# Moving expert turns between the phases of a decoder layer's second half

## What is computed

```python
f = lb + (1 - lb) * sigmoid(fa)
oa, S_new = hgrn_chunked(q, 1 - f, i, log(f), S0)
ya = (rms_norm(oa) * silu(ga)) @ w_branch_a
yb = merged_window_attention(q, k, v, caches) @ w_branch_b
x = x + g1 * ((sigmoid(gA) * ya + sigmoid(gB) * yb) @ w_out)
n2 = rms_norm(x) * (1 + sc2) + sh2
...
act = gelu(einsum('td,thkd->thk', n2, u[eidx]))
x = x + g2 * einsum('thk,thkd->td', g * act, v[eidx])
```

## Time and profile before

| | |
|---|---|
| median of three runs | 4373.25 us |
| the profiled execution's own time | 4375.05 us |
| its span, first to last instruction | 4373.3 us |
| mean granted TensorE clock | 0.824 |
| PE, PEld busy | 3063.8 us (70%), 1663.8 us (38%) |
| DVE busy | 2572.8 us (59%) |
| ACT busy | 1940.2 us (44%) |
| POOL busy | 1446.6 us (33%) |
| bytes moved, mean rate | 1454.06 MB, 332 GB/s |

### The profile page before, as it was taken

The page is one execution under the profiler, slowest core; times in us unless marked ns, Lnnn a source line. Parts: engine busy times, 40 slices in busy tenths (PEclk is TensorE's granted clock), DMA queues, the critical chain, the costliest instruction groups (busy, mean ns, idle before and its releaser), DMA issues. The chain is left out here.

```text
span 4373.3 us, 46875 instructions
## 1 busy us (share of the span) xinstructions
PE 3063.8 (70%) x14244; PEld 1663.8 (38%) x14244; DVE 2572.8 (59%) x6558; ACT 1940.2 (44%) x6708; POOL 1446.6 (33%) x1174
## 2 busy tenths in 40 slices
PE   7999877784898998566654686885555556555556
PEld 5677754641553446344432464551111111111111
DVE  2362335377566755584654545467667766766774
ACT  2123431045457844574542225445455555545554
POOL 4453102352332333232211113335244344334432
PEclk9998889886999999666876797887777776777879
DMA  7434245388999999787999988999999999999997
GB/s 281 185 142 138 83 142 179 112 354 335 364 406 377 422 421 401 287 334 274 382 360 361 344 308 312 381 368 386 403 420 420 415 409 420 420 404 419 417 407 308
DMA packets 313887, 1454.06 MB, mean 332 GB/s; under 512 B 41609, under 2 KB 102977, under 8 KB 165282
## 3 DMA queue, kind: packets, MB, share of 16 engines
q0 software_dynamic: 152064, 1107.36, 62.6%
q1 hardware_dynamic: 147118, 336.43, 21.7%
q10 hardware_dynamic: 14452, 7.26, 0.6%
HBM read 1383.55 MB, written 74.57 MB: 333 GB/s over the span
## 5 line engine op out<-in xcount | busy, mean ns | idle before, releaser
L3249 POOL DMA_INDIRECT uv_ring<-in_peer_uv,pick_idx x736 | 794.9, 1080 | 1853.4 <-PE expert_acc L3421 1355.2
L3421 PE MATMUL expert_acc<-uv_ring,diag 128*32 128x512 f32 (+1 forms) x2888 | 714.4, 781 | 424.8 <-ACT diag L3386 373.3
L3344 DVE SCALAR_TENSOR_TENSOR uv_ring<-uv_ring,n_pairs 128x1024 f32<-128x1024 f32 x534 | 651.2, 1232 | 410.0 <-DMA uv_ring<-in_peer_uv,pick_idx 339.1
L3373 ACT ACTIVATE gelu_cube<-dots_now 128x2 f32<-128x2 f32 x528 | 105.7, 200 | 1017.8 <-DVE uv_ring L3344 589.9
L3421 PEld LDWEIGHTS expert_acc<-uv_ring,diag 128*32 128x32 f32 (+1 forms) x2888 | 154.8, 149 | 886.0 <-ACT diag L3386 544.6
L3381 ACT ACTIVATE pick_weight<-gelu_tanh,pick_share 128x1 f32<-128x1 f32 x1056 | 350.9, 379 | 23.1 <-ACT pick_share L3378 4.1
L3421 PE MATMUL expert_acc<-uv_tail,diag 128*64 128x512 f32 x608 | 215.4, 847 | 171.6 <-ACT diag L3386 150.3
L3344 DVE SCALAR_TENSOR_TENSOR uv_ring<-uv_ring,n_more 128x1024 f32<-128x1024 f32 x202 | 243.7, 1222 | 144.8 <-DMA uv_ring<-in_peer_uv,pick_idx 111.6
L997 PE MATMUL h_acc_q<-in_w_all_q,n_all_q 128*128 128x512 f32 x640 | 285.1, 601 | 4.0 <-DVE h_stage_q L971 3.7
L3376 ACT ACTIVATE gelu_tanh<-gelu_cube,dots_now 128x1 f32<-128x1 f32 x1056 | 253.3, 287 | 16.3
L3378 ACT ACTIVATE pick_share<-dots_now,pick_prob 128x1 f32<-128x1 f32 x1056 | 245.4, 280 | 0.0
(11 more groups left out here) (491 smaller groups left out, 5876.7 us busy)
## 6 DMA issues: line engine op xcount, KB each, us to landing
in_w_p<-in_w_in SPq DMA_DIRECT2D x34, 1024.0 KB, 7.4
in_w_all_q<-in_w_in SPq DMA_DIRECT2D x17, 2048.0 KB
ada_w<-in_w_ada SPq DMA_DIRECT2D x10, 2048.0 KB, 8.2
past_keys_q<-in_past_keys SPq DMA_DIRECT2D x16, 1024.0 KB
uv_ring<-in_peer_uv,pick_idx POOLq DMA_INDIRECT x736
shared_room_q<-in_past_values SPq DMA_DIRECT2D x10, 1024.0 KB
score_pair<-scores SPq DMA_DIRECT2D x66, 128.0 KB
wq_raw_p<-in_peer_wq SPq DMA_DIRECT2D x16, 512.0 KB, 5.8
```

Source lines behind the costliest of these rows:

```text
L3249: pool.indirect_dma_start(self.rows_of(part, s), None, self.x["peer_uv"][0], bass.IndirectOffsetOnAxis(ap=self.idx[:, q % 2, 2 * half + s, ...
L3344: ins = dve.scalar_tensor_tensor(out=row, in0=row, scalar=1.0, in1=n2[:, s if tile < LAST_TILE else 0, :], op0=ALU.mult, op1=ALU.mult, acc ...
L3373: link(act.activation(self.cube[:], dots, ACT.Square))
L3421: ins = pe.matmul(self.acc[s * w:(s + 1) * w, c, :], self.diag[:, of % DIAGS, t, 0:w], rows, start=first, stop=last)
```

## The change

Four numbers of `PACE` are changed. The recurrence's and the attention's are raised, the merge's and the branches' lowered:

```diff
-PACE = {norm_phase: 1.2, project_phase: 1.8, hgrn_phase: 1.5, attention_phase: 1.7, merge_phase: 1.25, branch_phase: 1.2, out_phase: 1.2,
+PACE = {norm_phase: 1.2, project_phase: 1.8, hgrn_phase: 1.79, attention_phase: 2.06, merge_phase: 0.8, branch_phase: 0.17, out_phase: 1.2,
         query_phase: 1.18}
```

## The result

| | before | changed |
|---|---|---|
| median | 4374.6 us (20 runs, 4363.57 to 4388.17) | 4391.39 us (20 runs, 4374.01 to 4403.02) |
| ratio | 1 | 1.0033, interval 1.0022 to 1.0045 |
| the profiled execution, span | 4373.3 us | 4383.5 us |

The change costs 0.33%, some 14 us, where 7 us less had been forecast. The loss is within the 0.5% that the chances call no change, and above the range's upper end of 4388.

What follows compares the result with a forecast made beforehand. The prediction saw different limits per stretch, with DMA-bound closing experts, so only idle DMA time ahead of them could be won. Terms 15 + 32 - 26 - 28 = -7 us gave a median of 4366 us, range 4342 to 4388.

Steps and rivals of the forecast that it cites:

- Recurrence, +15: Recurrence: 5 more parts, priced mostly by DVE's multiplications, lengthen it by 15 us; ends 9 and 26.
- Attention, +32: Attention: 6 more parts at 5.18 us of gathers plus n2 rows lengthen it by 32 us; ends 23 and 38.
- Its rival, that the attention takes parts in: Attention: its hole and idle time absorb added parts, giving 23 us growth and 4346 us in all; chance 0.22.
- Merge, -26: Merge: 5 fewer parts and n2 loads remove 28.5 us of DMA time, shortening it by 26 us.
- I leave 2.5 us for more of that: Merge: allowance of 2.5 us for its own chain of loads, spread and product leaving the DMA engines idle.
- The low end of -16: Merge: its DMA share falls to 0.9 on the remaining 130 us, losing 13 us, so it shrinks only 16.
- Branches, -28: Branches: PE's diagonal waits (22.6 us) and three sums (8.9 us) go, shortening it by 28 us; ends -32 and -18.
- the last group, put at 3.5 us: Branches: the copy ahead of the last block's sigmoid, without four gathers beside it, costs 3.5 us.
- the rival: Branches: copies take as long without gathers and hold the sigmoids, so only 10 us go; 4384 us; chance 0.10.
- the rule of the Trainium skill: Branches: starting a DMA takes its engine little time; by it the branches would give 8.9 us instead of 28.
- From the output on, nothing: Output product and later phases: part counts are 79 before and after, so they are costed at nothing.
- The slower rival: Attention's last jobs: the n2-row wait moves there and drains the DMA queue, adding 15 us; 4401 us in all; chance 0.10.

Runs made afterwards that it cites:

- e5: Changed kernel with four slots instead of two for the samples' new states, removing DVE's wait for stores; ratio 1.0046 to the kernel before.
- e3: Kernel before with only the first half of the change: 5 parts moved from merge to recurrence; ratio 0.9996.
- e9: Kernel before with 5 of the branches' 7 parts moved to the recurrence, merge keeping 15 and attention 29; ratio 0.9971.
- e1: Changed kernel with the branches' pace 0.1442 instead of 0.17, restoring the old order from the output product on; ratio 1.0017 to the kernel before.
- e7: Kernel before with the copies of keys and values taken off ACT in the branches and issued by SP during the output's product; ratio 1.0007.
- e12: Kernel before with only the branches' pace raised to 1.226, giving output, norm and query the changed kernel's order; ratio 1.0016.
- e4: Kernel before with only the second half of the change: 6 parts moved from branches to attention; ratio 1.0028.
- e14: Kernel before with parts set to 36 beside recurrence, 29 attention, 13 merge and 1 branches; ratio 0.9975.

## Why the prediction was wrong

By its terms, against the profile before:

- **Recurrence, +15: measured +27.6**, above the upper end of 26, and 247 to 250 in all executions with 33 parts and two slots for states. What the term priced by DVE was the whole gather and more: the stretch moved 81.0 MB (249.12 us at 325 GB/s) in place of 67.1 (221.4 at 303), 13.9 more, where 5 parts are 10.5. Two things were not counted: in the samples' tile DVE waited 18.8 us for stores, and gathers run ahead, so that the stretch carried work of the next one. Taking the first away won nothing (e5). In e3 the second comes back: its attention moved 97.3 MB (271.06 us at 359) in place of 100.6 (282.6 at 356), 3.3 less, some 8 us; the rest of its -11.5 may be spread. As a term the size was wrong; as a loss it is not where the time went.
- **Attention, +32: +30.9.** The price held, 5.18 us a part and the n2 rows: with 35 parts the share is 0.97. The closeness is partly luck, since this stretch spreads by 11 to 14 us, and has 5 us of new idle behind the n2 rows. Its rival, that the attention takes parts in, came out in small only: the idle time at its start went from 14 us (two slices at 0.70 and 0.16) to 7 (three at 0.90, 0.81 and 0.73), but new idle took its place.
- **Merge, -26: -23.2.** Within its ends, but by luck, for here the reasoning failed: "I leave 2.5 us for more of that" was 14 us. What hid it is that more work left than was counted: the merge's busy DMA time fell by 37 us (155.87 x 0.97 to 132.64 x 0.86) in place of 28.5. The parts were the merge's cover. e9, with 15 parts behind the same recurrence, needs 145 us at a share of 1.00, e1 132 with 10: the five parts were worth 13 us, not 28.5. The low end of -16 named this case (a share of 0.9) and took it for the exception.
- **Branches, -28: -31.3.** Right, with its cause: the diagonals' waits are gone, and e7 wins nearly as much (28.7) by taking the copies away. Of the six groups of small copies the prediction named three; the fifth, in two pieces of 5.04 and 2.01 us, took less than its neighbours. It laid the long ones to the gathers beside them, but without gathers the time still grows with the large copy ahead, and the last group, put at 3.5 us, took 8.55. That it cost nothing is luck: it held the last sigmoid, as the rival said, which ended 0.2 us before PE's last products. On the rule of the Trainium skill (DMA: Bandwidth & Descriptors, "Issuing engines are not separate DMA queues"), that a start usually takes its engine little time, the runs agree with the trace of before and not with the rule: on SP four small copies took 17.55 us to issue (e7), on ACT 10.04.
- **From the output on, nothing: +5.8 us in the query.** This step failed outright. The count of turns in a phase was compared, not their places; the fraction of a part that is due at the end of the branches moved them. e12 prices this alone at 0.16%, e1 takes it back.
- **The slower rival.** Its wait for n2 rows is there (17.7 us in the changed kernel, 19.85 in e4), and so is what it feared, an idle stretch behind the wait. But that is 5 us in the changed kernel's attention, not 15; in e4 the wait falls at the merge's start and the merge is 10.6 us longer.

In idle DMA time (a stretch's length times what its share lacks to 1, from the windows above and the earlier trace rows, each good to some 2 us) the forecast was 11 us less in the recurrence, 2 less in the attention, 2.5 more in the merge, 3 more in the branches and none in the query. Measured are 9.7 less, 1.9 less, 13.9 more, 5.4 less and 8.6 more. So two steps failed, the merge's and the query's.

By the ratios, half of the loss of 0.33% is the query's order (0.16% by e12, and as much goes in e1, each give or take 0.15). What is left in e1, 0.17% or 7 us where 7 less were forecast, fits the merge's idle time. This half is argued from shares and from e9 and e14, where the merge keeps 15 and 13 parts and the kernel is faster than before; no run takes parts from the merge alone, as they must go somewhere. By halves of the change, the second alone costs 0.28% (e4), the first alone nothing (e3); that the shares add up to a little more than the whole is within the intervals. Not settled is why the attention spreads by 11 to 14 us between executions of one order.

## What to carry to other kernels

Before work is taken out of a stretch, ask what that stretch will do without it: a stretch whose DMA engines are full may be full only because of the guest work, and its own chain shows when the guest leaves (here the share fell from 0.97 to 0.86). Judge a move by all neighbouring stretches together, since transfers that run ahead shift time over the boundaries. Where a schedule counts in fractions, a change of one number moves every later turn; compare the later order itself, not only its counts.

## What was not expected of the hardware

Issuing small DMAs held whichever engine did it, ACT (10.04 us for four, with no new gathers beside) or SP (17.55 us, with four gathers just issued). Without gathers beside, four small copies took longer the larger the copy ahead of them: 2.78, 4.21 and 10.04 us behind 128, 512 and 1024 tokens. Eight loads of n2 rows took SP 12.08 us in e4, at the merge's start behind loads of values, and 4.59 in the changed kernel, in the attention. And waits under full DMA engines could be worth nothing: the 18.8 us of DVE's waiting went (e5) without any gain.
